# Two attentions of a fused two-block kernel: scores masked and reduced in one pass, meta keys first, values for two query blocks at once

## The reference

```python
def sink_softmax(s, mask, sink):
    s = jnp.where(mask, s.astype(jnp.float32), NEG_INF)
    m = jnp.maximum(jnp.max(s, axis=-1, keepdims=True), sink)
    p = jnp.exp(s - m)
    return p / (jnp.sum(p, axis=-1, keepdims=True) + jnp.exp(sink - m))
...
    s = jnp.einsum('bkgnqd,bknsd->bkgnqs', q_blk, k_band)
    ...
    p = sink_softmax(s, mask, sink_b[None, :, :, None, None, None])
    o_real = jnp.einsum('bkgnqs,bknsd->bkgnqd', p.astype(v.dtype), v_band)
```

## Time and profile before

| What | us |
|---|---|
| median of 3 runs | 1800.12 |
| the runs | 1798.22, 1800.12, 1810.4 |
| span of the profiled execution (first to last instruction) | 1796.1 |
| busy: PE / DVE / ACT in that span | 1746.7 / 1066.6 / 715.0 |
| mean granted TensorE clock | 0.994 of full |

### The profile page before, as it was taken

How to read it: one execution, slowest core, us unless ns; L and a number is a source line. 1 busy time by engine, 2 the same in 40 slices (tenths; PEclk the granted TensorE clock), 3 DMA queues, 4 the chain that set the end, 5 groups by cost and what they waited for, 6 DMA issues and landing times.

```text
span 1796.1 us, 31908 instructions
## 1 busy us (share of the span) xinstructions
PE 1746.7 (97%) x12556; PEld 1413.9 (79%) x12556; DVE 1066.6 (59%) x1883; ACT 715.0 (40%) x1151; POOL 21.2 (1%) x26
## 2 busy tenths in 40 slices
PE   9999999999999999999999999998999999999996
PEld 8999989799999999998899998998953333333332
DVE  7775565787665877669787656867672222222223
ACT  5344553463444544455643446957431101110110
POOL 0000000100000000000000001000020000000000
PEclk9999999999999999999999999999999999999998
DMA  6545333444453355531245645443779999999996
GB/s 240 183 167 203 122 140 142 63 148 176 173 208 136 141 187 184 203 133 69 95 164 187 219 164 188 152 150 115 327 276 394 428 429 427 426 428 429 427 427 258
DMA packets 42339, 409.71 MB, mean 228 GB/s; under 512 B 5304, under 2 KB 5304, under 8 KB 7056
## 3 DMA queue, kind: packets, MB, share of 16 engines
q1 hardware_dynamic: 40032, 402.21, 57.4%
q0 software_dynamic: 1936, 5.79, 1.6%
q10 hardware_dynamic: 288, 0.52, 0.1%
HBM read 405.87 MB, written 2.63 MB: 227 GB/s over the span
## 4 chain that ended last, share of the span: by engine, by line
PE 82%; DVE 11%; DMA 5%; ACT 1%; issue 1%; DVEq 0%; SPq 0%; ACTq 0%
PE ps L598 81%; DMA soon<-w_gate_up 4%; DVE w_lo L1719 2%; PE ps L602 2%; DMA raw<-w_units 1%; DVE h L1825 1%; DVE x_lo L1781 1%; DVE h L1829 1%; DVE rs L1761 1%; DVE arena L2095 1%; DVE small L2101 0%; DVE arena L2126 0%; DVE x_lo L1779 0%; DVE small L2100 0%; DVE zg L1789 0%
## 5 line engine op out<-in xcount | busy, mean ns | idle before, releaser
L598 PE MATMUL ps<-x_hi,w_hi 128*128 128x256 f32 (+1 forms) x2144 | 617.3, 288 | 14.0 <-DVE x_lo L1779 5.0
L598 PE MATMUL ps<-x_lo,w_hi 128*128 128x256 f32 (+1 forms) x2144 | 610.7, 285 | 0.0
L598 PE MATMUL ps<-x_hi,w_lo 128*128 128x256 f32 (+1 forms) x2144 | 609.2, 284 | 0.0
L1719 DVE TENSOR_TENSOR w_lo<-raw,w_hi 128x1024 fp32r<-128x1024 f32 (+1 forms) x352 | 441.3, 1292 | 84.5 <-ACT w_hi L1282 84.3
L598 PEld LDWEIGHTS ps<-x_hi,w_hi 128*128 128x128 f32 x2144 | 403.9, 188 | 26.1 <-issue 9.6
L1282 ACT ACTIVATE w_hi<-raw 128x1024 fp32r<-128x1024 f32 (+1 forms) x352 | 379.2, 1111 | 95.2 <-PE ps L598 68.1
L598 PEld LDWEIGHTS ps<-x_hi,w_lo 128*128 128x128 f32 x2144 | 405.9, 189 | 0.0
L598 PEld LDWEIGHTS ps<-x_lo,w_hi 128*128 128x128 f32 x2144 | 404.9, 189 | 0.2
L598 PE MATMUL ps<-hid_hi,w_hi 128*128 128x272 f32 (+1 forms) x720 | 206.0, 286 | 0.7 <-DVE hid_lo L1781 0.3
L598 PE MATMUL ps<-hid_hi,w_lo 128*128 128x272 f32 (+1 forms) x720 | 204.6, 284 | 0.0
L598 PE MATMUL ps<-hid_lo,w_hi 128*128 128x272 f32 (+1 forms) x720 | 204.0, 283 | 0.0
(11 more groups left out here) (331 smaller groups left out, 1959.5 us busy)
## 6 DMA issues: line engine op xcount, KB each, us to landing
raw<-w_units SPq DMA_DIRECT2D x144, 1024.0 KB, 4.8
soon<-w_gate_up SPq DMA_DIRECT2D x34, 2048.0 KB, 18.3
late<-w_gate_up SPq DMA_DIRECT2D x30, 2048.0 KB, 18.6
raw<-w_out_units SPq DMA_DIRECT2D x32, 1408.0 KB, 6.0
soon<-w_down SPq DMA_DIRECT2D x16, 2048.0 KB, 18.9
late<-w_down SPq DMA_DIRECT2D x16, 2048.0 KB, 18.6
bias_rows<-kT POOLq DMA_DIRECT2D x1, 1536.0 KB, 33.4
cst<-table SPq DMA_DIRECT2D x1, 1448.0 KB, 11.7
```

What stands on the lines that cost most here:

```text
L598: return nc.tensor.matmul(out_ap, lhsT, rhs, start=start, stop=stop, skip_group_check=True)
L1719: v.tensor_tensor(part(w_lo, c, 0, n), raw_slot(u, j * n, n), part(w_hi, c, 0, n).bitcast(F32), ALU.subtract).then_inc(lo_made, 1)
```

## The change

Meta keys stand first in `kT`, so that a query block's scores are one product per head. One VectorE instruction adds the mask to the scores in PSUM, scales by -0.125, writes the result and gives the minimum over the row, started with the negated sink; ACT's exponential gets a scale of -1. The sinks are negated once ahead of the loop. In the second attention a copy of the four minima carries the signal. The values of a key block are multiplied with both query blocks at once; the transposed blocks are laid out for that, and the first bank holds both query blocks of both heads. The second attention's bias is multiplied by 8 beforehand, since the scale now comes after the addition. Keys are rotated in place and written in two parts.

```diff
@@ -95,9 +95,9 @@
-    c["swa0"][:, :P] = own
-    c["swa1"][:, :P] = np.where(t > s, 0, NEG)
-    c["swa1"][:, P:2 * P] = own
+    c["swa0"][:, META:] = own
+    c["swa1"][:, META:META + P] = np.where(t > s, 0, NEG)
+    c["swa1"][:, META + P:] = own
@@ -211,24 +211,16 @@
+        NEG_SINK = 66
...
-        SWA_SEGS = (((0, P, 0), (P, META, SEQ)), ((0, P, 0), (P, P, P), (2 * P, META, SEQ)))
-        MOBA_SEGS = (((0, P, 0),), ((0, P, 0), (P, P, P)))
-        SWA_TURNS = ((P, 512, ((0, 0, 0), (1, 0, P), (2, 0, 2 * P), (2, 1, 3 * P))), (P, 256, ((3, 0, 0), (3, 1, P))),
-                     (META, 512, ((0, 1, 0), (1, 1, P), (2, 2, 2 * P), (3, 2, 3 * P))))
-        MOBA_TURNS = ((P, 256, ((0, 0, 0), (1, 0, P))), (P, 512, ((2, 0, 0), (2, 1, P), (3, 0, 2 * P), (3, 1, 3 * P))))
-
-        def turned_at(turns):
-
-            at, base = {}, 0
-            for rows, n, parts in turns:
-                for u, s, c in parts:
-                    at[u, s] = base + c
-                base += n
-            return at
+        SWA_KEYS = {"first": (META, P), "second": (META + P, P), "meta": (0, META)}
+        MOBA_KEYS = {"first": (0, P), "second": (P, P)}
+        SWA_TURNS = ((P, 512, "first", ((0, 0), (2, P), (1, 2 * P), (3, 3 * P))), (P, 256, "second", ((2, 0), (3, P))),
+                     (META, 512, "meta", ((0, 0), (2, P), (1, 2 * P), (3, 3 * P))))
+        MOBA_TURNS = ((P, 512, "first", ((0, 0), (2, P), (1, 2 * P), (3, 3 * P))), (P, 256, "second", ((2, 0), (3, P))))
@@ -883,35 +875,33 @@
-            def attend(names, groups, first, pbs, pTs, second, row, q_of, k_of, v_of, segs, turns, done, values=None,
+            def attend(names, groups, first, pbs, pTs, second, row, q_of, k_of, v_of, places, turns, done, values=None,
...
                 S, TT, V = (plan[x] for x in names)
-                t_at = turned_at(turns)
...
                     for n in range(2):
-                        for at, size, key in segs[n]:
-                            for b in range(2):
-                                hs = slice(64 * b, 64 * b + 64)
-                                c = n * second + at
-                                m = mm(banks[b][:, c:c + size], q_of(g, hs, n), k_of(g, hs, key, size), True, True)
-                                if n and at == segs[n][-1][0]:
-                                    m.then_inc(full[ts[b][0]], 1)
+                        a, size = (second, row - second) if n else (0, second)
+                        for b in range(2):
+                            hs = slice(64 * b, 64 * b + 64)
+                            m = mm(banks[b][:, a:a + size], q_of(g, hs, n), k_of(g, hs, size), True, True)
+                            if n:
+                                m.then_inc(full[ts[b][0]], 1)
...
                 def turns_of(g):
-                    for i, (rows, cols, parts) in enumerate(turns):
+                    for i, (rows, cols, keys, parts) in enumerate(turns):
...
-                        for u, s, c in parts:
+                        at, size = places[keys]
+                        for u, c in parts:
...
-                            if s == 0:
+                            if i == 0:
...
-                            at, size, key = segs[n][s]
@@ -922,12 +912,14 @@
-                    for n in range(2):
-                        for s, (at, size, key) in enumerate(segs[n]):
-                            for b in range(2):
-                                a = t_at[2 * n + b, s]
-                                m = mm(bank[64 * b:64 * b + 64, n * P:(n + 1) * P], v_of(g, b, key, size),
-                                       pTs[g % 2][0:size, a:a + P], s == 0, s == len(segs[n]) - 1)
+                    base = 0
+                    for i, (rows, cols, keys, parts) in enumerate(turns):
+                        wide = cols // 2
+                        for b in range(2):
+                            a = base + b * wide
+                            m = mm(bank[64 * b:64 * b + 64, 2 * P - wide:2 * P], v_of(g, b, keys, places[keys][1]),
+                                   pTs[g % 2][0:rows, a:a + wide], i == 0, i == len(turns) - 1)
+                        base += cols
@@ -960,9 +952,10 @@
-                   lambda g, hs, key, size: kT[hs, g // 4, key:key + size],
-                   lambda g, b, key, size: vs[0:size, key // P, (2 * (g // 4) + b) * 64:(2 * (g // 4) + b) * 64 + 64],
-                   SWA_SEGS, SWA_TURNS, lambda g: pe.wait_ge(q_roped, g + 1), router_constants)
+                   lambda g, hs, size: kT[hs, g // 4, 0:size],
+                   lambda g, b, keys, size: vs[0:size, ("first", "second", "meta").index(keys),
+                                               (2 * (g // 4) + b) * 64:(2 * (g // 4) + b) * 64 + 64],
+                   SWA_KEYS, SWA_TURNS, lambda g: pe.wait_ge(q_roped, g + 1), router_constants)
@@ -1063,9 +1056,10 @@
-                   lambda g, hs, key, size: b_mk[hs, g * SEQ + key:g * SEQ + key + size],
-                   lambda g, b, key, size: b_mv[0:size, key // P * 512 + (2 * g + b) * 64:key // P * 512 + (2 * g + b) * 64 + 64],
-                   MOBA_SEGS, MOBA_TURNS, moba_ready, values, 4, heads_out)
+                   lambda g, hs, size: b_mk[hs, g * SEQ:g * SEQ + size],
+                   lambda g, b, keys, size: b_mv[0:size, (keys == "second") * 512 + (2 * g + b) * 64:
+                                                 (keys == "second") * 512 + (2 * g + b) * 64 + 64],
+                   MOBA_KEYS, MOBA_TURNS, moba_ready, values, 4, heads_out)
@@ -1492,7 +1486,7 @@
                         p = pbs[g % 3][:, a:a + (row - second if n else second)]
-                        e = nc.scalar.activation(p, p, ACT.Exp, bias=small[:, at + u:at + u + 1],
+                        e = nc.scalar.activation(p, p, ACT.Exp, bias=small[:, at + u:at + u + 1], scale=-1.0,
@@ -2044,8 +2038,10 @@
-                then(v.tensor_tensor(kT[:, i, :], tile(s_kraw, i, TA), C("cos"), ALU.mult))
-                then(v.tensor_tensor(kT[:, i, :], kT[:, i, :], tile(s_krot, i, TA), ALU.add))
+                k, r = tile(s_kraw, i, TA), tile(s_krot, i, TA)
+                then(v.tensor_tensor(k, k, C("cos"), ALU.mult))
+                v.tensor_tensor(kT[:, i, META:TA], k[:, 0:SEQ], r[:, 0:SEQ], ALU.add)
+                did(v.tensor_tensor(kT[:, i, 0:META], k[:, SEQ:TA], r[:, SEQ:TA], ALU.add))
@@ -2091,22 +2087,20 @@
-                        for c, w, mask in masks_of(g, b):
-                            e = v.scalar_tensor_tensor(pb[:, b * row + c:b * row + c + w], bank[:, c:c + w], 0.125, mask,
-                                                       ALU.mult, ALU.add)
+                        for n in range(2):
+                            u = 2 * n + b
+                            a, size = (second, row - second) if n else (0, second)
+                            most = small[:, NEG_SINK + 4 * g + u:NEG_SINK + 4 * g + u + 1] if sinks else -NEG
+                            e = v.tensor_tensor_reduce(pb[:, b * row + a:b * row + a + size], bank[:, a:a + size],
+                                                       masks_of(g, b)[n], -0.125, most, ALU.add, ALU.min,
+                                                       small[:, at + u:at + u + 1])
...
-                    p3 = pb.rearrange("p (b t) -> p b t", b=2)
-                    did(v.tensor_reduce(small[:, at:at + 2], p3[:, :, 0:second], AX, ALU.max))
-                    then(v.tensor_reduce(small[:, at + 2:at + 4], p3[:, :, second:row], AX, ALU.max))
                     if sinks:
...
-                        then(v.tensor_tensor(small[:, at:at + 4], small[:, at:at + 4], sk, ALU.max))
-                        then(v.tensor_scalar(small[:, at:at + 4], small[:, at:at + 4], -1.0, None, ALU.mult))
...
                     else:
-                        v.tensor_scalar(small[:, at:at + 4], small[:, at:at + 4], -1.0, None, ALU.mult)\
-                            .then_inc(neg_max, 1)
+                        v.tensor_scalar(small[:, at + 4:at + 8], small[:, at:at + 4], 1.0, None, ALU.mult).then_inc(neg_max, 1)
@@ -2152,8 +2146,8 @@
-            at = C_COLS["swa0"][0]
-            attend(("ss",), 8, 0, a_p, P + META, SWA_ROW, lambda g, b: ((0, SWA_ROW, cst[:, at:at + SWA_ROW]),), True,
+            then(v.tensor_scalar(small[:, NEG_SINK:NEG_SINK + 32], W("sinks"), -1.0, None, ALU.mult))
+            attend(("ss",), 8, 0, a_p, P + META, SWA_ROW, lambda g, b: (C("swa0"), C("swa1")), True,
@@ -2244,8 +2238,8 @@
                 for i in range(4 * j, 4 * j + 4):
-                    last = v.tensor_tensor(b_bias[:, i * SEQ:(i + 1) * SEQ], b_bias[:, i * SEQ:(i + 1) * SEQ], C("ninf"),
-                                           ALU.add)
+                    last = v.scalar_tensor_tensor(b_bias[:, i * SEQ:(i + 1) * SEQ], b_bias[:, i * SEQ:(i + 1) * SEQ], 8.0,
+                                                  C("ninf"), ALU.mult, ALU.add)
@@ -2310,7 +2304,7 @@
```

(2 more changed lines are left out.)

## The result

The changed kernel has a median of 1793.09 us (10 runs, 1790.31 to 1794.34) beside 1799.11 for the kernel before (10 runs, 1797.69 to 1810.4): 6.0 us less by the medians. The record's ratio is 0.9949, with a 95% interval of 0.9935 to 0.9963, which is 7 to 12 us; the ratio of the two medians, 0.9967, lies just outside it. A second set of runs of the changed kernel (a8) stands at 1791.90 beside 1800.63, 8.7 us less. So the gain is 6 to 9 us. The forecast was 1794.0, a gain of 6.0. Its profiled execution has a span of 1789.6 us and a time of 1791.5; what lies outside the span is 1.8 to 2.0 us in every run of either kernel, so half of the 4.0 us of distance that I kept was scatter.

A forecast was written before the change was run, and what follows sets the result against it. PE (4.15 us a group) and DVE (4.07) were taken to bound the first attention together. Gains of 4.4 us there and 1.6 in the second gave 6.0, span 1790.1, plus 4.0 to the median: 1794.0 us, range 1788.5 to 1801.

The forecast's parts named there:

- Which engines bound: First attention's loop: PE at 4.15 us a group and DVE at 4.07 bind together, ACT next at 3.49.
- DVE's passes: First attention: four reducing passes cost 1.82 us a group in place of 2.55 removed; DVE's group becomes 3.37.
- the accumulator at 0.10 us: DVE's reducing passes: writing out each minimum costs 0.10 us, priced from ACT's accumulator reads, 0.40 a group.
- the equation: Streaming price of DVE's passes from the old mask passes: 1.06 ns a column plus 0.064 us an instruction.
- The pointer's 0.07: First attention's DVE passes: reading the sink by per-partition pointer costs 0.06 to 0.07 us each, 0.28 a group.
- the first rival: DVE's reducing pass streams at half rate, its group 4.25 us, no gain in first attention, kernel 1800 us; 13%.
- PE's scores and transposes: First attention: scores fall to 0.84 us a group by columns (0.49 by instruction count); transposes stay at 1.24.
- PE's values: First attention: values fall from 1.69 to 1.35 us a group, the middle of 1.01 by count and 1.69 by columns.
- The loop: First attention: DVE 3.37, PE 3.43, ACT 3.49 plus 0.1 waits gives 3.6 us a group, 3.85 gained over seven intervals.
- Head and tail: First attention's ends: 0.55 us gained at the first maxima, 0.7 at the last values, 0.7 lost to PE's low clock.
- Second attention: Gain of 1.6 us: 1.3 from DVE, half of 2.5 counted, and 0.3 from two value products with fewer instructions.
- Behind: After the attentions: the whole gain passes on, since last weights and expert transfers start from the chain, not fixed times.

The follow-up runs named there:

- e1: Kernel before with only the VectorE half (reducing passes and sign), TensorE's products as before: loop 4.15 us, first attention 42.63, median 1796.95, ratio 0.9975.
- e2: Changed kernel with VectorE's old mask passes and reductions, so TensorE's half alone: loop 4.07 us, first attention 40.50, median 1801.38, ratio 1.000.
- e5: Changed kernel without the meta keys' value products in the first attention: loop 3.38 us, first attention 33.42; one run.
- e4: Changed kernel with score products cut back into three pieces, 20 instructions a group for 8: scores 1.31 us, loop 3.94, median 1796.82, ratio 0.9974.
- e3: Changed kernel with value products cut back to one per query block and key piece, new order kept: values 1.40 us, loop 3.55, median 1791.75.
- e7: Changed kernel with ten value products in the order of the kernel before: values 1.69 us, loop 3.83; one run.
- e9: Changed kernel with ten value products, meta keys last, but the two heads by turns: values 1.39 us, loop 3.53; one run.
- e6: Changed kernel with the second attention's scaling for the last two groups moved from ACT to VectorE: second attention 49.23 us, median 1790.49, ratio 0.9940.
- e12: Kernel before with only the VectorE half, run again unedited: first attention 39.56 us, median 1797.60, ratio 0.9973.

## Why the prediction was right, point by point

- **Which engines bound.** Right, and shown by e1, e2 and e5: PE 4.15, DVE 4.07, ACT third. What I didn't see is that this holds for the steady part only. At the head of the first attention, and in the last two groups, where PE makes no scores, the chain ran through DVE (and ACT's exponents) without PE's full work beside it, so the vector half alone gains 2.0 us.
- **DVE's passes.** "I take 1.82 us" a group was too high: they took 1.52. The term that was mis-sized is the accumulator at 0.10 us for each pass. It has a record of 0.08 us, but the next pass starts with it, and 128 columns follow one another at 0.21 us, where the equation without it gives 0.20. The pointer's 0.07 was right: by the columns of the passes without one (0.21 and 0.34), 144 and 272 columns would be 0.23 and 0.36; with it they are 0.29 and 0.42. The half rate of the first rival is refuted: 128 more columns cost 0.13 us, 1.0 ns a column. The Trainium skill (VectorE: DVE Perf Modes, section "Two Vector instructions with no wait between them") counts such a pass as two instructions, and two show in the trace; the second costs next to nothing.
- **PE's scores and transposes.** 0.84 and 1.24 forecast, 0.90 and 1.25 measured; by columns was the right choice for the wide pieces, and by instruction for the narrow ones (e4), where the weight loads fill the time. In the second attention, where nothing was narrow, the shorter count gave nothing (1.58 us for 1.61), as the price by columns says.
- **PE's values.** 1.35 forecast, 1.38 measured, for a wrong reason. "By count" and "by columns" were both wrong as causes: the width gave 0.02, the 0.29 came from two changes between 128 and 16 rows that the new order spares (e3, e7, e9). The middle of two wrong prices lay near it by luck. Where there are no such changes, in the second attention, 8 merged instructions take 0.87 us for 0.88, and my 0.3 us there didn't come.
- **The loop.** 3.6 forecast, 3.52 measured, but not by the way I had it: I took ACT's 3.49 and 0.1 of waits between three engines, and it is PE's work without a wait, 0.90 + 1.25 + 1.37; ACT would have allowed 3.38 (e5), and DVE 3.1 for my 3.37. From the first scaling to the last DVE took 27.17 us before (833.23 to 860.40) and 23.30 after: 3.87 for my 3.85. That agrees by luck in part: the first two steps, where PE hasn't a whole group's work yet (its first values start at 836.73), gained 1.1 us each, the next four 0.6 each, and the last lost 0.8, because before it had been short.
- **Head and tail.** The 0.55 at the head was mis-sized, 1.62 measured (8.13 us from the first scores to the first scaling, 6.51 after): two groups' maxima stood ahead of the first scaling, not one; after, ACT's exponents end last there (829.29 to 831.31 in the chain). The sum was slipped too: 0.73 less 0.16 is 0.57. The tail gave 0.96 for 0.7. The 0.7 us for the clock didn't come; where a fall came, it cost 0, 0.5 or 1.8 (a8, e6, e3).
- **Second attention.** 1.3 for DVE, counted as half of the work removed, was 1.14, all of it VectorE's half.
- **Behind.** The gain passed on: the wait for the last projection's weights and the expert stage moved with it, but for 1.4 us that a fall of the clock took in this execution. The prediction has no such term. The distance from span to median, kept at 4.0, was 3.5.

4.4 + 1.6 = 6.0 forecast. Measured are 6.45 + 1.16, less 1.4 behind and 0.1 ahead, 6.1 at the router's stage and 6.5 over the span; 6.0 between the two medians, 8.7 in the second set of runs (a8). Each of the two main errors, the head (1.1) and the clock (0.7), was larger than the error over the span (0.5), and both lay on the same side; the 1.4 behind, which was not forecast, and the 0.4 missing in the second attention set them off. The mechanism was right, the closeness of the number is luck in part.

## What to carry to other kernels

Where two engines stand within 2% of each other in a loop, price the ends of the loop apart from its steady part: there the two don't both have a full group's work, and a change of the one that the chain runs through gains at once. Between matrix products count the changes of the operand's rows before the instructions: putting the 16-row products side by side was worth as much as the whole shortening of the values. When the bound has moved to a third engine, look in the same stretch for one that waits, and hand it a piece: here that gave 3.2 us in the traces, beside the change's 6 to 9.

## What the runs showed that I had not expected

- A VectorE pass that adds a mask, scales and takes a minimum runs at 1.0 to 1.1 ns a column from PSUM and SBUF, as the plain pass does, and its accumulator's read (a record of 0.08 us) is hidden under the next pass.
- A change between value operands of 128 and of 16 rows on PE cost 0.15 us each (e7 beside e9, 1.69 and 1.39 us with two changes more), and shows as a pause of 0.17 us between two weight loads.
- A score product narrower than 128 columns costs its weight load of 128 columns, 0.06 us an instruction (1.19 us for twenty in e4), not its width.
- A start flag in a bank of PSUM ends the open sum beside it, in other columns of the same rows (e3); with the flag on the first product alone both sums are whole (e9). Beside this flag the two differ only in the order of the heads. The Trainium skill says the same (PSUM — Partial Sum Buffer, section "The four PSUM rules"): the first product clears the state of the whole bank in the quadrants it writes.
- TensorE's granted clock fell from 1.00 to 0.50, from 2.4 to 1.2 GHz, at recurring places (near 28, 240, 832, 1092, 1237 to 1256 and 1271 to 1320 us), no place in every execution, for 3.4 to 10.2 us each. Just ahead of the falls near 832 us PE had worked on with pauses of 0.7 us at most (e6); the longest came in the kernel in which it had no pause at all (e1), but the same kernel had a short one too (e12), and the changed kernel had a fall there or none (a8, after).
